# Other starting offsets within 512 bytes for the two halves of the down projections' input and for the turned queries

## The reference

```python
def conv_ffn(h, w_up, conv_w, conv_b, w_down):
    gu = h @ w_up
    g = gu[..., :D_FF]
    u = gu[..., D_FF:]
    ...
    return (jax.nn.silu(g) * u) @ w_down

def swiglu(x, w13, w2):
    gate, up = jnp.split(x @ w13, 2, axis=-1)
    return (jax.nn.silu(gate) * up) @ w2
```

## Time and profile before

| | us |
|---|---|
| median of 3 runs | 2125.82 |
| lowest and highest | 2122.11 and 2129.02 |
| the profiled execution, its own time | 2125.66 |
| its span, first to last instruction | 2123.9 |
| TensorE busy with matmuls | 2067.6 (97%) |
| VectorE busy | 1433.9 (68%) |
| ScalarE busy | 1055.2 (50%) |
| mean granted TensorE clock | 0.993 |

### The profile page before, as it was taken

One profiled execution on the slowest core, in us unless ns is written; L12 is line 12 of the kernel. 1 busy time (PEld: TensorE's weight loads), 2 busy tenths in 40 slices (PEclk: granted clock), 3 DMA queues, 4 the chain that ended last, 5 costly groups with the idle time before them and its releaser, 6 DMA issues.

```text
span 2123.9 us, 34246 instructions
## 1 busy us (share of the span) xinstructions
PE 2067.6 (97%) x14836; PEld 1801.3 (85%) x14836; DVE 1433.9 (68%) x1652; ACT 1055.2 (50%) x1256; POOL 155.4 (7%) x119
## 2 busy tenths in 40 slices
PE   8899999999999999999999999999999999999998
PEld 7888888988888888998778888888889977788887
DVE  7966766567765664876766776476558576678654
ACT  4545554655643553455544455345435564444542
POOL 1000000000001000330000010020005200002000
PEclk9799999999999999999999999999999999999999
DMA  7254655435555665563402466566546533135653
GB/s 186 40 169 153 198 189 172 156 119 179 179 188 189 197 199 178 186 206 126 139 23 100 156 205 195 188 189 198 180 161 217 197 119 119 43 119 167 210 189 129
DMA packets 259789, 342.45 MB, mean 161 GB/s; under 512 B 23383, under 2 KB 169469, under 8 KB 259639
## 3 DMA queue, kind: packets, MB, share of 16 engines
q1 hardware_dynamic: 254272, 329.95, 47.7%
q0 software_dynamic: 2768, 9.08, 1.5%
q10 hardware_dynamic: 2599, 1.23, 0.5%
HBM read 338.14 MB, written 2.10 MB: 160 GB/s over the span
## 4 chain that ended last, share of the span: by engine, by line
PE 77%; DVE 14%; ACT 4%; DMA 3%; issue 1%; POOL 0%; ACTq 0%; SPq 0%; DVEq 0%
PE acc L1969 10%; PE acc L1971 10%; PE acc L1970 10%; PE trp L2139 9%; PE acc L2139 7%; DVE w_lo L1244 5%; PE trp L2140 4%; PE acc L2140 4%; PE acc L1985 3%; PE trp L1969 2%; PE trp L1971 2%; PE trp L1970 2%; ACT w_hi L750 2%; PE acc L2034 1%; PE acc L2186 1%
## 5 line engine op out<-in xcount | busy, mean ns | idle before, releaser
L1244 DVE TENSOR_TENSOR w_lo<-raw,w_hi 128x2048 fp32r<-128x2048 f32 (+1 forms) x312 | 721.4, 2315 | 400.3 <-ACT w_hi L750 398.5
L750 ACT ACTIVATE w_hi<-raw 128x2048 fp32r<-128x2048 f32 (+1 forms) x312 | 586.2, 1880 | 526.3 <-PE acc L1971 182.0
L2139 PE MATMUL trp<-xT,w_hi 128*128 128x512 f32 x960 | 339.5, 398 | 0.8 <-DVE w_lo L1244 0.8
L2139 PE MATMUL acc<-xT,w_hi 128*128 128x512 f32 x768 | 271.3, 397 | 0.0
L2140 PE MATMUL trp<-xT,w_lo 128*128 128x256 f32 x960 | 268.9, 280 | 0.0
L2139 PEld LDWEIGHTS trp<-xT,w_hi 128*128 128x128 f32 x960 | 180.3, 188 | 45.6 <-issue 1.7
L2140 PE MATMUL acc<-xT,w_lo 128*128 128x256 f32 x768 | 215.1, 280 | 0.0
L1969 PE MATMUL acc<-w_hi,hT_hi 128*128 128x512 f32 x528 | 205.5, 389 | 0.0
L1970 PE MATMUL acc<-w_lo,hT_hi 128*128 128x512 f32 x528 | 205.5, 389 | 0.0
L1971 PE MATMUL acc<-w_hi,hT_lo 128*128 128x512 f32 x528 | 205.4, 389 | 0.0
L1969 PE MATMUL acc<-xT,w_hi 128*128 128x256 f32 x704 | 199.9, 284 | 3.5 <-DVE w_lo L1244 3.4
(11 more groups left out here) (436 smaller groups left out, 3430.8 us busy)
## 6 DMA issues: line engine op xcount, KB each, us to landing
raw<-in_ffn_w SPq DMA_DIRECT2D x184, 512.0 KB
raw<-in_w_in SPq DMA_DIRECT2D x60, 1024.0 KB
raw<-in_ffn_w_up SPq DMA_DIRECT2D x88, 512.0 KB
raw<-in_ffn_w SPq DMA_DIRECT2D x40, 1024.0 KB
raw<-in_ffn_w_down SPq DMA_DIRECT2D x20, 1024.0 KB
raw<-in_ssm_w_glu SPq DMA_DIRECT2D x16, 512.0 KB
raw<-in_kv_w SPq DMA_DIRECT2D x8, 1024.0 KB
raw<-in_w_branch_a SPq DMA_DIRECT2D x8, 1024.0 KB
```

Source lines behind the costliest of these rows:

```text
L750: A(w_hi[:, p % SPL, 0:kt, :], raw[:, p % RAW, 0:kt, :], ACT.Copy).then_inc(hi_ready, 1)
L1244: V_.tensor_tensor(w_lo[:, p % SPL, 0:kt, :], raw[:, p % RAW, 0:kt, :], w_hi[:, p % SPL, 0:kt, :].bitcast(F32), ALU.subtract).then_inc(lo_ ...
L2139: mm(tile, w_hi[:, p % SPL, k, c], xT[:, k0 + k], start=i == k == 0, stop=False, skip_group_check=True)
```

## The change

Two paddings are added and one is cut; nothing else differs. The same instructions are issued in the same order on every engine, with other addresses.

```diff
         s2 = ExitStack()
-        sb("hT_offset", [P, 104], F32, s2)
+        sb("hT_offset", [P, 40], F32, s2)
         hT_hi = sb("hT_hi", [P, FT, SEQ], F32R, s2)
+        sb("hT_rest_offset", [P, 80], F32, s2)
         hT_lo = sb("hT_lo", [P, FT, SEQ], F32R, s2)
         hbuf = sb("hbuf", [P, 2, 2, SEQ], F32, s2)
         folds = sb("folds", [P, 2, 4, SEQ], F32, s2)
...
         s3a = ExitStack()
+        sb("qx_offset", [P, 8], F32, s3a)
         qx = sb("qx", [P, KT, 2, SEQ], F32R, s3a)
         s3a.close()
```

## The result

| | before | after |
|---|---|---|
| median, us (5 runs each, taken together) | 2125.4 | 2132.57 |
| lowest and highest | 2122.11 and 2129.02 | 2130.34 and 2133.58 |
| profiled execution's span | 2123.9 | 2130.8 |

The ratio after to before is 1.0031, 95% interval 1.0021 to 1.0042. That is slower by 6.6 us by the ratio, 7.2 by the two medians, just past the 6.4 us (0.3%) from which the prediction counts a change.

What follows compares the result with a forecast made beforehand. TensorE was taken to bound the kernel, through the distance between matmul starts in the down projections. The terms, 0 + 0 + 0 + 0 on the profiled execution's 2125.7 us, gave 2125.7 us; the range was 2109 to 2133.

Steps and rivals of the forecast that it cites:

- What bounds the kernel: TensorE, busy 2067.6 of 2123.9 us; a nanosecond on each of 1584 down-projection matmuls is worth 1.58 us.
- The sign set for being wrong: Second down projection: the 264 starts take under 58.6 or over 60.7 us.
- The term for the stationary operands: Down projections, `hT_hi` to 384 and `hT_lo` to 192: 0, with one step of 5.3 us to either side.
- The bounds: Down projections' stationary operands: at best -17.9 us on TensorE, at worst +6.6 ns per matmul, +10.5 us.
- The lower bound: Down projections: at best the whole 11.3 ns per matmul beyond plain float32 go, -17.9 us on TensorE.
- the collision theory: Down projections: equal offsets make the streams collide; unlike ones save up to 14.9 us, 2110.8 us; chance 0.30.
- The slower rival: Down projections: new offsets bring in the merged projections' uneven rhythm, at worst +10.5 us, 2136.2 us; chance 0.16.
- A shift of rhythm elsewhere: Merged up projections of five later blocks move to the 346.7 ns rhythm: 9.5 us less, 2116.2 us; chance 0.04.
- The writers at 0: ScalarE's copies and VectorE's differences into moved buffers, beside up projections: costed at 0; 10% slower adds 9 us of work.
- the padding at 0: The added padding: no instruction touches it, 0.
- `qx` at 0: Queries' 192 matmuls with `qx` as moving operand, 224 to 256: 0; one 3.3 ns step would be 0.6 us.
- Where a gain is lost: Ends of down projections: the first's share of a gain is lost, the second passes it on; best case -14.9 us.

Runs made afterwards that it cites:

- e12: Kernel before with `hT_lo` alone moved to 192 (`hbuf` and `folds` follow it): 2131.53 against 2125.34 us, ratio 1.0031.
- e3: Kernel before with another (`hT_hi`, `hT_lo`) offset pair in each down projection, weights at 128: 59.64 to 61.37 us per 264 starts.
- e6: Kernel before with `raw`, `w_hi`, `w_lo`, `xT` 64 bytes later, at 192, and an `hT` pair per down projection: 59.64 to 61.37 us per 264 starts.
- e10: Kernel before with feed-forward input in its own tensor `x_ffn`, at 64, 96, 224, 240, 256, 288 by layer: 2121.34 against 2125.25 us.
- e9: Kernel before with feed-forward input in its own tensor `x_ffn`, at 128, 144, 160, 176, 192, 208 by layer: 2121.27 against 2125.25 us.
- e8: Kernel before with `xT` and what lies behind it at 192, weights at 128, an `hT` pair per down projection: 2134.61 against 2126.05 us.
- e2: Kernel before with only the padding ahead of `qx` (`qx` at 256): 2125.51 against 2125.59 us, ratio 0.9999.
- e11: Kernel before with `x_ffn` at 160 in all six layers and `qx` at 160: 2118.89 against 2125.34 us, ratio 0.9966.

## Why the prediction was right or wrong

**What bounds the kernel:** right. TensorE's start-to-start distance in the down projections was the lever, 1.58 us per nanosecond: 4.3 ns more gave 6.8 us. The sign set for being wrong, over 60.7 us for the 264 starts, came by a hair (60.78).

**"I take 0, because the nearest row, `qx` at an unlike offset, kept its mean exactly": this is the step that failed.** The term for the stationary operands was put at 0 and was 6 x 1.14 = 6.8 us, all of it from `hT_lo` 64 bytes past the weights (`e12`, and (128, 192) in `e3`); for `hT_hi` at 384 the 0 was right. The row did not speak for it, for three reasons. `qx` is the moving operand and `hT_lo` the stationary one. The form was 256 columns wide and not 512. (The up projections have other good distances than the down projections; since role and form differ together there, which of the two makes the difference is not shown.) And one distance was taken to speak for all: 96 bytes gave 120.0 ns for `qx`, 128 gave 118.7, and 32 gave 116.7 where the weights lay at 192 (`e6`). The equal means were a coincidence of one pair. Nor was `qx` "the one pair of buffers of this kernel with unlike offsets": `bdw_hi` at 192 against `xT` at 128 is another, 64 bytes apart like `hT_lo` after the change, and it came every 117.5 ns. The text put the 2.5 ns to the 119.9 of `xT` down to the 16 columns. With 128 columns at that same distance (`e10`, 64) the products came every 118.3 ns, against 120.6 for 128 in the same layer of `e9`, so most of the 2.5 ns seems to go with the distance. The trace had a row, then, in which unlike offsets changed the distance of starts, if to the quicker side.

**The bounds:** they held for this change, but +6.6 ns is not the worst that offsets can do. It is what both tensors 64 bytes on give (1.73 us a projection is 6.6 ns), by luck, since it came from another loop; both at 224 give 7.5 ns (61.61 us). The change had 4.3, since only one of its tensors sits 64 bytes on. The lower bound, 11.3 ns gone, was never approached: none of the 36 passes of `e3` to `e8` was under 59.61 us, so the collision theory, to which I gave 0.30, falls for the down projections. There equal offsets were the best case, not the worst. In the 256-wide products of the up projections it has something to it: 120 ns went down to 114.4 and 113.7 at 144 and 240. What the 11.3 ns of the down projections are stays open.

**The slower rival** named the mechanism, with 0.16: "the new offsets bring the uneven rhythm into the down projections", and the rhythm is indeed 228, 229, 236. Its reason was half right. It held both moves to matter; `hT_hi` at 384 is the same as at 128, since the pattern repeats after 256 bytes. The trace had no row on the period, and the text should have said so: a move by 256 may be no move.

**A shift of rhythm elsewhere** (0.04) came, but to the slower side: the last layer's merged projections, 1.8 us more, made up for by another stretch. The price of this rival was too high: the last of the five later blocks was in the quick rhythm already (99.96 us), so four were left, 7.6 us and not 9.5.

**The writers at 0, the padding at 0:** right, 614 and 784 ns again, `e2` without effect. **`qx` at 0:** 0.25 us less, under its own 0.6.

**Where a gain is lost:** the first projection's chain behaved as told for a loss, which came through whole. For a gain `e11` shows more of a loss than I had: at the end of the second projection, where VectorE had 0.48 us to spare, its chain came to be the one that ends last too, and the lower clock behind the gap added to it.

**The chances:** 0.16 for slower was too low for what the trace had. The earlier trace rows showed that the same stream can run 3.3 ns apart; a value chosen from one calm row should not have carried half of the weight. That the time still lies within the range, by 0.4 us, is because the range had been drawn up to 2133 for the milder half of the slower case.

## What to carry to other kernels

With back-to-back float32r matmuls that each load new weights, the start of the stationary operand relative to the moving one, modulo 256 bytes, was worth up to 3% of the stream's time here (61.61 for 59.64 us), with not one wait to show for it. Read it from the start-to-start distance, and where a loop runs several times in a kernel give each pass its own offset: one run is then a table. `hT`, which is loaded as weights, did best at distance 0 from what moves past it; `x_ffn`, which only moves, did best at 16 to 32 bytes past the weights (and at 160, for the merged pairs). The period of 256 bytes was tried for `hT` alone. A gain on TensorE then has to be followed to the next engine, since the weights' pipeline may end last.

## What was not expected of the hardware

- The rhythm of a stream of matmuls depends on the distance of its two operands modulo 256 bytes: 59.64 us at 0, 60.06 at -16, 60.19 at -64, 61.11 at 128, 61.36 or 61.37 at 16, 32, 64, -32 and -96, 61.61 at 96, for 263 steps with both tensors moved alike. It does not depend on where both lie (six pairs within 0.01 us).
- The parts of two stationary tensors do not add: `hT_lo` alone 64 bytes back costs 1.14 us, `hT_hi` alone 0.60, both 0.55.
- The same distance can give two values: 118.7 (`xT` and `qx`) and 120.0 ns (`x_ffn`) for the 256-wide products at 128 bytes, 348.9 and 353 for the merged pairs with `xT` at 192. What picks the rhythm, and why the curve is uneven, stays open; distances under 16 bytes were not tried.
- After one gap of 2.01 us in a full stream TensorE's granted clock averaged 0.69 over the stretch of 4 us that began 1.5 us later.
